# Stick-breaking attention: a capping copy, three ScalarE passes, doubled q and k, and a projection in thirds

## The reference, cut to what matters

```python
z = jnp.einsum('bhqd,bhkd->bhqk', q_blk, kh).astype(jnp.float32) * inv_sqrt   # 1/8
mask = key_pos[None, :] < q_pos[:, None]
log_1m_beta = jnp.where(mask, jax.nn.log_sigmoid(-z), 0.0)
suffix = lax.cumsum(log_1m_beta, axis=3, reverse=True) - log_1m_beta
a = jnp.where(mask, jnp.exp(jax.nn.log_sigmoid(z) + suffix), 0.0)
o = jnp.einsum('bhqk,bhkd->bhqd', a, vh)
```

## Time and profile before

| | |
|---|---|
| median of 3 runs | 3356.91 us (3354.5 to 3360.6) |
| the profiled execution | 3357.51 us; span of the profile 3355.7 us |
| TensorE busy | 3145.6 us (94%), mean granted clock 0.949 |
| VectorE busy | 1762.8 us (53%) |
| ScalarE busy | 825.7 us (25%) |
| GpSimd busy | 1135.5 us (34%) |
| stick-breaking stage | from 2033.5 us (first scores) to about 2385 us (last v product) |

### The profile page before, as it was taken

The page is one execution under the profiler, slowest core; times in us unless marked ns, Lnnn a source line. Parts: engine busy times, 40 slices in busy tenths (PEclk is TensorE's granted clock), DMA queues, the critical chain, the costliest instruction groups (busy, mean ns, idle before and its releaser), DMA issues.

```text
span 3355.7 us, 41230 instructions
## 1 busy us (share of the span) xinstructions
PE 3145.6 (94%) x14878; PEld 2540.1 (76%) x14878; DVE 1762.8 (53%) x2127; ACT 825.7 (25%) x1491; POOL 1135.5 (34%) x780
## 2 busy tenths in 40 slices
PE   7998998788989999999889998999999899999997
PEld 6885667677878888888678876666777688888886
DVE  4464445654267777777742006778322544444446
ACT  2223553111331111111220005666312311111111
POOL 4321002332753333333553321111236633333333
PEclk9998999998999999999999999885899899999999
DMA  3200000000422222222221200000113111111111
GB/s 111 57 19 13 9 2 1 1 0 14 149 82 81 88 81 82 81 83 80 94 65 45 59 28 18 13 13 0 49 58 119 51 50 50 50 50 44 50 44 63
DMA packets 211168, 171.57 MB, mean 51 GB/s; under 512 B 13367, under 2 KB 186702, under 8 KB 211086
## 3 DMA queue, kind: packets, MB, share of 16 engines
q1 hardware_dynamic: 158430, 135.34, 13.2%
q10 hardware_dynamic: 52656, 35.13, 3.5%
HBM read 162.06 MB, written 8.39 MB: 51 GB/s over the span
## 4 chain that ended last, share of the span: by engine, by line
PE 82%; DVE 8%; POOL 4%; ACT 2%; issue 2%; DMA 1%; SPq 0%; DVEq 0%; ACTq 0%; POOLq 0%
PE ps L852 12%; PE ps L854 12%; PE ps L853 12%; PE ps L1175 7%; PE ps L1176 7%; PE ps L1177 7%; PE ps L1022 4%; PE ps L1318 2%; PE ps L987 2%; PE ps L967 2%; PE ps L1298 2%; PE ps L871 1%; PE ps L873 1%; PE ps L872 1%; DVE sb_weights L2255 1%
## 5 line engine op out<-in xcount | busy, mean ns | idle before, releaser
L214 POOL TENSOR_SCALAR slab_hi<-raw 128x1024 fp32r<-128x1024 f32 (+1 forms) x236 | 267.2, 1132 | 1424.1 <-PE ps L854 581.6
L852 PE MATMUL ps<-act_hi,slab_hi 128*128 128x512 f32 x1600 | 630.6, 394 | 4.5 <-DVE o_feat_lo L1812 1.7
L853 PE MATMUL ps<-act_lo,slab_hi 128*128 128x512 f32 x1600 | 625.9, 391 | 0.0
L854 PE MATMUL ps<-act_hi,slab_lo 128*128 128x512 f32 x1600 | 625.8, 391 | 0.0
L217 POOL TENSOR_TENSOR slab_lo<-raw,slab_hi 128x1024 fp32r<-128x1024 f32 (+1 forms) x236 | 579.6, 2456 | 19.7
L2168 DVE TENSOR_TENSOR acc<-ps,acc 128x512 f32<-128x512 f32 x512 | 339.5, 686 | 201.4 <-PE ps L1177 201.4
L1175 PE MATMUL ps<-slab_hi,hid_hi 128*128 128x512 f32 x1024 | 404.1, 395 | 7.1 <-DVE hid_lo L2159 3.8
L1176 PE MATMUL ps<-slab_hi,hid_lo 128*128 128x512 f32 x1024 | 400.0, 391 | 0.0
L1177 PE MATMUL ps<-slab_lo,hid_hi 128*128 128x512 f32 x1024 | 399.4, 390 | 0.0
L852 PEld LDWEIGHTS ps<-act_hi,slab_hi 128*128 128x128 f32 x1600 | 303.1, 189 | 68.5 <-DVE o_feat_lo L1812 1.9
L854 PEld LDWEIGHTS ps<-act_hi,slab_lo 128*128 128x128 f32 x1600 | 302.3, 189 | 64.1
(11 more groups left out here) (322 smaller groups left out, 4753.1 us busy)
## 6 DMA issues: line engine op xcount, KB each, us to landing
raw<-in_w_in SPq DMA_DIRECT2D x56, 512.0 KB, 3.8
w_ada<-in_w_ada ACTq DMA_DIRECT2D x48, 512.0 KB, 4.1
raw<-in_w_out SPq DMA_DIRECT2D x32, 512.0 KB, 3.7
raw<-in_w_up SPq DMA_DIRECT2D x32, 512.0 KB, 4.0
raw<-in_w_down SPq DMA_DIRECT2D x32, 512.0 KB, 3.5
raw<-in_w_mlp_in SPq DMA_DIRECT2D x32, 512.0 KB, 4.0
raw<-in_w_mlp_out SPq DMA_DIRECT2D x32, 512.0 KB, 3.5
x_tok<-in_x SPq DMA_DIRECT2D x8, 512.0 KB, 6.7
```

The costliest lines, as they stand in the source:

```text
L214: pool.tensor_scalar(self.hi[s][:, 0:width], self.raw[r][:, 0:width], 1.0, 0.0, ALU.mult, ALU.add)\
L852: pe.matmul(o, hi[:, w], a_hi[:, k, cols], start=(k == 0), stop=False)
L853: pe.matmul(o, hi[:, w], a_lo[:, k, cols], start=False, stop=False)
L854: mm = pe.matmul(o, lo[:, w], a_hi[:, k, cols], start=False, stop=(k == nk - 1))
```

## The change

All four pairs are written out (no hardware loop). In words:

- VectorE copies the scores out under a minimum with 40 (all but the last block) and, for the last block, a minimum with the table, now 40 and -1e30, straight from PSUM. The factor 1/8 goes into ScalarE's copy of q. In step s VectorE caps item s + 1 and then finishes item s.
- Since z is at most 40, exp z can't overflow: ScalarE makes softplus as Exp and Ln, and max(z, 0) is not added. TensorE transposes the arguments, and ScalarE takes Exp on the way out of PSUM, in place of the copy. The lag of the transposes is 2 and that of the v products 3.
- q2 and k2 are doubled: ScalarE copies the projection straight into the pair's own buffer, and GpSimd's copies go.
- A projection's 24 products stand as 9, 9 and 6 at the ends of three steps in turn (steps 0 to 11). ScalarE takes a finished one at the start of steps 3, 6, 9 and 12.

```diff
-SB_PROJECT = (3, 6, 9, 12)
+SB_THIRDS = (range(0, 3), range(3, 6), range(6, 8))
-SB_LAG_ARG, SB_LAG_EXP, SB_LAG_TURN, SB_LAG_PV = 1, 2, 3, 4
+SB_LAG_TURN, SB_LAG_PV = 2, 3
+SB_Z_CAP = 40.0
...
-    c[:, C_KEYCAP:C_KEYCAP + P] = np.where(k < r, 3e38, -1e30)
+    c[:, C_KEYCAP:C_KEYCAP + P] = np.where(k < r, SB_Z_CAP, -1e30)
...
-        q2, k2 = sb("q2_feat", 17, [P, SEQ]), sb("k2_feat", 21, [P, SEQ])
+        q2 = [sb(f"q2_feat{i}", kb, [P, SEQ]) for i, kb in enumerate((17, 81))]
+        k2 = [sb(f"k2_feat{i}", kb, [P, SEQ]) for i, kb in enumerate((21, 85))]
...
-            sb_stage(0)
-            with pool.Fori(0, SB_PAIRS - 1) as i:
+            for i in range(SB_PAIRS):
                 for j in range(2):
-                    R8.split(pool, 2 * i + 2, i + 1, j)
-                sb_stage(i + 1)
+                    R8.split(pool, 2 * i, i, j)
...
-                panel(R8.hi[j], R8.lo[j], act_hi, act_lo, (7, 7), KD, (sem("panel_half"), R8.used), (h,))
+                o, cols = ps[:, 7, :], slice(h * HALF, (h + 1) * HALF)
+                for k in ks:
+                    w = slice(k * P, (k + 1) * P)
+                    pe.matmul(o, R8.hi[j][:, w], act_hi[:, k, cols], start=(k == 0), stop=False)
+                    pe.matmul(o, R8.hi[j][:, w], act_lo[:, k, cols], start=False, stop=False)
+                    mm = pe.matmul(o, R8.lo[j][:, w], act_hi[:, k, cols], start=False, stop=(k == KD - 1))
...
                 if s % NT == 0:
-                    pe.wait_ge(sem("sb_qk_done"), 4 * i + 2 * (s // NT) + 2)
-                pe.wait_ge(sem("sb_z_done"), SB_ITEMS * i + s + 1)
+                    pe.wait_ge(sem("proj_read"), 4 * i + (4 * MLA_HEADS + s // NT + 4))
+                pe.wait_ge(sem("sb_z_copied"), SB_ITEMS * i + s + 1)
...
-                pe.wait_ge(sem("sb_weights_done"), SB_ITEMS * i + s + 1)
+                pe.wait_ge(sem("sb_arg_done"), SB_ITEMS * i + s + 1)
...
-                    if s in SB_PROJECT and not last:
-                        sb_project(i + 1, SB_PROJECT.index(s))
+                    if s < 12 and not last:
+                        sb_project(i + 1, s // 3, SB_THIRDS[s % 3])
...
-                act.copy((q2_next, k2_next)[j][:, h * HALF:(h + 1) * HALF], ps[:, 7, :]).then_inc(sem("proj_read"), 1)
+                act.activation((q2, k2)[j][i % 2][:, h * HALF:(h + 1) * HALF], ps[:, 7, :], ACT.Copy, scale=(z_scale, 1.0)[j])\
+                    .then_inc(sem("proj_read"), 1)
...
-                ach.link(act.activation(l, sb_z[s % 2][:, 0:n], ACT.Abs))
-                ach.link(act.activation(l, l, ACT.Exp, scale=-1.0))
+                act.activation(l, z, ACT.Exp).then_inc(sem("sb_exp_done"), 1)
+                act.wait_ge(sem("sb_exp_done"), SB_ITEMS * i + s + 1)
                 act.activation(l, l, ACT.Ln, bias=1.0).then_inc(sem("sb_ln_done"), 1)
...
-                    act.copy(sb_at[g % 2][:, 0:w], ps[:, 4 + g % 2, 0:w]).then_inc(sem("sb_at_done"), 1)
-
-            def sb_exp(i, s):
-                a = sb_w[s % SB_SLOTS][:, 0:(s // 2 + 1) * P]
-                act.wait_ge(sem("sb_arg_done"), SB_ITEMS * i + s + 1)
-                act.activation(a, a, ACT.Exp).then_inc(sem("sb_weights_done"), 1)
+                    act.activation(sb_at[g % 2][:, 0:w], ps[:, 4 + g % 2, 0:w], ACT.Exp).then_inc(sem("sb_at_done"), 1)
...
-                    if late := lagged(i, before, s, SB_LAG_EXP, SB_ITEMS):
-                        sb_exp(*late)
+                    if s in (3, 6, 9, 12) and not last:
+                        sb_take_projection(i + 1, s // 3 - 1)
                     sb_softplus(i, s, before)
                     if late := lagged(i, before, s, SB_LAG_TURN, SB_ITEMS):
                         sb_weights_out(*late)
-                    if s - 1 in SB_PROJECT and not last:
-                        sb_take_projection(i + 1, SB_PROJECT.index(s - 1))
...
-                ch.link(dve.tensor_scalar(z[:, 0:n], ps[:, 2 * (s % 2):2 * (s % 2) + 2, :].rearrange("p b n -> p (b n)")[:, 0:n],
-                                          z_scale, None, ALU.mult))
-                dve.tensor_tensor(z[:, t * P:n], z[:, t * P:n], consts[:, C_KEYCAP:C_KEYCAP + P], ALU.min)\
-                    .then_inc(sem("sb_z_done"), 1)
+                if n > P:
+                    dve.tensor_scalar(z[:, 0:n - P], scores[:, 0:n - P], SB_Z_CAP, None, ALU.min)
+                dve.tensor_tensor(z[:, n - P:n], scores[:, n - P:n], key_cap, ALU.min).then_inc(sem("sb_z_copied"), 1)
...
-                ch.link(dve.scalar_tensor_tensor(l, z, 0.0, l, ALU.max, ALU.add))
                 ch.link(dve.tensor_tensor_scan(l[:, ::-1], l[:, ::-1], l[:, ::-1], 0.0, ALU.add, ALU.bypass))
```

More of the change, by code:

```diff
@@ L1321, in sb_outputs, with sb_pair @@
                     mm.then_inc(sem("sb_pv"), 1)
-            def sb_pair(i, before, last):
+            def sb_pair(i):
+                before, last = (i - 1 if i else None), i == SB_PAIRS - 1
                 for s in range(SB_ITEMS):
@@ L1336, in _ @@
             for n in range(4):
[L1337 removed]
+                sb_project(0, n, range(KD))
             sb_scores(0, 0)
[L1339 to L1343 removed]
+            for i in range(SB_PAIRS):
+                sb_pair(i)
+            pe.wait_ge(sem("sb_z_copied"), SB_ITEMS * SB_PAIRS + 2)
             merge_gate(R9, 1, 0, 0)
@@ L1711, in _ @@
             act.preload_act_table_set("natural_log_exp_and_others")
+            z_scale = float(SB_DIM) ** -0.5
             def sb_take_projection(i, n):
                 j, h = n // 2, n % 2
-                if n == 0 and not isinstance(i, int):
-                    act.wait_ge(sem("sb_qk_done"), 4 * i)
                 if h == 0:
@@ L1753, in sb_pair @@
                         sb_weights_out(*late)
-                    if s - 1 in SB_PROJECT and not last:
-                        sb_take_projection(i + 1, SB_PROJECT.index(s - 1))
             for n in range(4):
                 sb_take_projection(0, n)
-            sb_pair(0, None, False)
-            with act.Fori(0, SB_PAIRS - 2) as i:
-                ach.loop(i, 2 * SB_ITEMS)
-                sb_pair(i + 1, i, False)
-            ach.end(SB_PAIRS - 2)
-            sb_pair(SB_PAIRS - 1, SB_PAIRS - 2, True)
+            for i in range(SB_PAIRS):
+                sb_pair(i)
             for s in range(SB_ITEMS, SB_ITEMS + SB_LAG_TURN):
-                if s < SB_ITEMS + SB_LAG_EXP:
-                    sb_exp(SB_PAIRS - 1, s - SB_LAG_EXP)
                 sb_weights_out(SB_PAIRS - 1, s - SB_LAG_TURN)
@@ L2266, in sb_pair @@
                 for s in range(SB_ITEMS):
-                    sb_take(i, s)
-                    if late := lagged(i, before, s, SB_LAG_ARG, SB_ITEMS):
-                        sb_log_weights(*late)
+                    if s + 1 < SB_ITEMS:
+                        sb_cap_scores(i, s + 1)
+                    elif i + 1 < SB_PAIRS:
+                        sb_cap_scores(i + 1, 0)
+                    sb_log_weights(i, s)
                     if before is not None and s == SB_LAG_PV - 1:
@@ L2273, in sb_pair @@
                         sb_out(i, 0)
-            sb_pair(0, None)
-            with dve.Fori(0, SB_PAIRS - 2) as i:
-                ch.loop(i, 3 * SB_ITEMS)
-                sb_pair(i + 1, i)
-            ch.end(SB_PAIRS - 2)
-            sb_pair(SB_PAIRS - 1, SB_PAIRS - 2)
-            sb_log_weights(SB_PAIRS - 1, SB_ITEMS - SB_LAG_ARG)
+            sb_cap_scores(0, 0)
+            for i in range(SB_PAIRS):
+                sb_pair(i, i - 1 if i else None)
             sb_out(SB_PAIRS - 1, 1)
```

54 lines of the change are left out of this document (20 added, 34 removed).

## The result

The changed kernel took **3279.69 us** (median of 4 runs, 3273.44 to 3282.65) against 3358.05 us before (median of 4 runs beside them, 3354.50 to 3360.60): ratio 0.9765, 95% interval 0.9746 to 0.9784. The prediction was 3293 us, 13 us more, in a range of 3262 to 3325. The profiled execution took 3282.21 us; its span is 3280.3 us, 75.4 us less than before, and TensorE's mean granted clock 0.969 against 0.949.

What follows compares the result with a forecast made beforehand. It took TensorE to bound pairs 0 to 2 and the low clock pair 3: 191.6 + 74.7 = 266.3 us against 328.5 (-62.2), 2 us less behind the gate; 3357.5 - 64.2 - 0.6 = 3293 us, range 3262 to 3325.

Steps and rivals of the forecast that it cites:

- TensorE paces pairs 0 to 2 at 2.4 GHz: Pairs 0 to 2: TensorE's work sets the pace at the full clock, 191.6 us for the three with waits.
- One wait of 1.4 us at each pair's end: Pair boundaries: item 13's v products wait for ScalarE, behind item 15's exponentials, 1.4 us a boundary.
- VectorE 50 us a pair, the PSUM minimum 0.29: VectorE's work in each pair: 50 us built up, with 0.29 us for each masked block's minimum straight from PSUM.
- Exp out of PSUM as fast as the copy: ScalarE, transposed blocks: Exp takes the same time as the copy it replaces; at worst 11 us a pair more.
- GpSimd's splits hidden at steps 5 and 12: Weight splits for a later pair, run at steps 5 and 12: cost nothing; without cover 8.6 us a pair.
- ScalarE's passes and its waits cost nothing: All pairs: ScalarE's work, at most 42 us of a pair, hides beside TensorE's 65; added wait nothing, 18 us uncovered.
- D: Rival, pairs 0 to 2: v products still wait on ScalarE's copies, 9.3 us a pair, +28, so 3321 us; chance 0.10.
- Pair 3 falls to 1.2 GHz and takes 74.7 us: Last pair, no projection: the clock falls in steps 3 to 6, then steps 4 to 15 take 62.7 us; 74.7 in all.
- that idle share: Pair 3, steps 3 to 6: TensorE has 5.7 us of work in VectorE's 9.7, taken as losing the clock.
- rival A: Pair 3: the clock holds and VectorE paces steps 3 to 13, 48.3 us in place of 74.7, so 3267; chance 0.20.
- B: Rival, pairs 0 to 2: the clock falls at each pair's end as before, +38 us, so 3331; chance 0.17.
- C: Rival, whole stage: projection thirds never bring 2.4 GHz back, 444 us against 328.5, so about 3470; chance 0.04.

## Why the prediction came out, point by point

- *TensorE paces pairs 0 to 2 at 2.4 GHz*: right. 195.4 us against 191.6. The 3.8 us are mostly a term of the sum: I took the rate of eight-block items for all. In the changed kernel scores of two blocks take 0.62 us from start to start (0.31 a block, against 0.239), and TensorE is busy for 66.7 us of a pair, where the sum has 64.7.
- *One wait of 1.4 us at each pair's end*: it is there, for ScalarE, at 0.36 and 0.26 us:

```profile
2226.05 1.77 PE L1312 MATMUL ps<-v_tok,sb_weights_t 128*128 128x64 f32 x14 [0.36 <-ACT sb_weights_t L1731]
...
2229.28 1.77 PE L1312 MATMUL ps<-v_tok,sb_weights_t 128*128 128x64 f32 x14 [0.26 <-ACT sb_weights_t L1731]
```

- *VectorE 50 us a pair, the PSUM minimum 0.29*: 49.5 and 0.28. *Exp out of PSUM as fast as the copy*: 43.7 us in all for 96, against 42.6 for the 96 copies before. *GpSimd's splits hidden at steps 5 and 12*: right; TensorE waits nowhere for them, and one scan a pair takes 1 us more.
- *ScalarE's passes and its waits cost nothing*: right for the changed kernel (2.8 us of VectorE waiting, and D with its 9.3 us a pair is refuted), but the margin is thin: two passes more cost 38.3 us. ScalarE is busy 33.7 us of a pair, half of it; yet with five passes an item of steps 14 and 15 takes it some 5.3 us (5 x 1.06) and TensorE some 4.8 (8 x 0.596), both estimates from rows. A busy share over a pair does not show that.
- *Pair 3 falls to 1.2 GHz and takes 74.7 us*: **this step failed.** It took 63.3. I placed the fall in steps 3 to 6, since TensorE has less work there than VectorE, and weighed that idle share. But TensorE may run ahead of VectorE, and at step 3 VectorE was close behind it: scores of item 4 at 2237.96 us beside item 2's scan (2236.83), scores of item 11 at 2252.47 beside item 8's (2251.22). So it drew on the lag and ran from 2228.5 to 2257.3 us with waits of 0.26 us in all and kept 1.00, on attention alone. The fall has another cause, one that the prediction does not name, at step 11: the copy that stands late in VectorE's list. With the copy early or the wait filled, pair 3 takes 47.8 and 49.3 us (27.1 + 20.7, 27.0 + 22.3), which is the 48.3 of rival A; so A was the right account of pair 3, but for one wait. That the time came out 13 us from the forecast is in this part luck: 63.3 us lie between the forecast's 74.7 and A's 48.3 because the clock fell at another place, for another reason.
- The Trainium skill ("TensorE: Matmul & The Clock Gate", Part 4: PE-mode transpose) says that transposes do not count as work for the clock, and the prediction had A fail by it. The runs do not bear that out: scores, v products and transposes together held 1.00 for 27 us, and with the copy early for most of 47.8. No run shows a long stretch of transposes alone, so the page's statement itself is not tested. "HAM oscillation" in the Trainium skill, on the same page (keep an output's K tiles together, so that waits between them don't lose the clock), was set against the thirds. The runs agree that waits lose the clock. Thirds kept 1.00 where no wait stood between them, and whole projections were slower by 13.4 us of the stage.
- *B*: refuted for the change, and yet a clock that falls at each pair's end is what any of the three parts put back brings. *C*: refuted, and by its own case: where the clock had fallen at a pair's end, one third of 9 products brought it back.
- The total of -64.2 us came out as -75.4 in the profiled executions, most of the difference in pair 3: -11.4 there, +3.8 in pairs 0 to 2, and 3.6 us more outside the pairs than the 2 I had taken.

## What to carry to other kernels

Count a lag as a reserve that one engine builds up and the other uses, not as slack in each step, and look for the instruction that sits nearer to its reader than the lag allows: here one 0.69 us copy, a step too late, cost 16 us. Where a clock depends on gaps, put parts back singly before crediting any of them, and look in the trace for which gap came back: each of three parts cost 32 to 39 us, and one of them by a wait that the kernel before did not have. And compare a stage by its own rows: the length of the work in front of it varied by 14 us between these kernels' profiled executions, though TensorE's products there are the same.

## What the runs showed of the hardware

- Behind each wait of 1.64 to 4.05 us shown above TensorE went on at 1.2 GHz, at once or within 2 us; behind those of 0.36 and 0.26 us at a pair's end it kept 2.4 GHz. Not every wait of such a length costs the clock: in the changed kernel TensorE waited 1.67 us before 2319.56 us, ahead of the second gate's products, and the clock is 1.00 from 2313 to 2330.5 us; the same wait before the change (1.67 us before 2391.83 us) was followed by products 0.43 us apart.
- At 1.2 GHz, attention products alone did not bring the clock back in 73 us in which TensorE was busy for 72.95; at 2.4 GHz the same products kept it for 27 us, until the wait. In the stage of these runs the clock rose again only in a projection's products (whole or a third) or a gate's, or right behind them.
- A minimum of a PSUM block with an SBUF table takes 0.282 us over 128 columns, the time of a copy of the same block (0.29).
